# Attention: 1/sum applied by a diagonal moving operand in the transposes, eight diagonals a tile made by GpSimd and VectorE

## The reference

```python
s_loc = jnp.einsum('bnqkgd,bnjkd->bkgnqj', qb, kb) * scale      # 3 blocks of 128 keys around the query block
s_loc = jnp.where(valid, s_loc, NEG_INF)
s_ctx = jnp.einsum('bnqkgd,bjkd->bkgnqj', qb, kc) * scale       # 256 context keys
s_snk = sink_logits(sink, s_loc.shape[:-1] + (1,))
p = jax.nn.softmax(jnp.concatenate([s_loc, s_ctx, s_snk], axis=-1), axis=-1)
o = einsum(p_loc, vb) + einsum(p_ctx, vc)
```

## Time and profile before

| | |
|---|---|
| median of 3 runs | 3465.7 us (3460.85 to 3466.91) |
| the profiled execution's own time | 3464.97 us |
| its span | 3463.2 us |
| PE, PEld, DVE, ACT, POOL busy | 3005.9, 2458.5, 2095.8, 1792.2, 541.9 us |
| attention stage, first score to last product | 403.6 to 597.1 us |

### The profile page before, as it was taken

How to read it: one execution, slowest core, us unless ns; L and a number is a source line. 1 busy time by engine, 2 the same in 40 slices (tenths; PEclk the granted TensorE clock), 3 DMA queues, 4 the chain that set the end, 5 groups by cost and what they waited for, 6 DMA issues and landing times. The chain is left out here.

```text
span 3463.2 us, 59847 instructions
## 1 busy us (share of the span) xinstructions
PE 3005.9 (87%) x24750; PEld 2458.5 (71%) x24750; DVE 2095.8 (61%) x2213; ACT 1792.2 (52%) x2017; POOL 541.9 (16%) x250
## 2 busy tenths in 40 slices
PE   6599887996799999999999948997929999999993
PEld 2488643452688888788888836774529999999993
DVE  0422375234566666666666645873357888888884
ACT  2411145232555555555555545884336777777773
POOL 1011043001011111210102004561030000000000
PEclk8699889997899999999999969998959999999997
DMA  7211100227778787777788621102247999999995
GB/s 327 75 37 37 55 1 21 85 91 296 274 264 273 263 275 268 259 258 264 270 274 268 239 81 52 40 31 92 93 174 272 362 380 354 354 387 358 354 353 178
DMA packets 137950, 726.07 MB, mean 210 GB/s; under 512 B 10708, under 2 KB 13524, under 8 KB 109828
## 3 DMA queue, kind: packets, MB, share of 16 engines
q1 hardware_dynamic: 125064, 684.99, 52.6%
q0 software_dynamic: 12288, 37.75, 4.6%
q10 hardware_dynamic: 384, 0.24, 0.0%
HBM read 680.90 MB, written 42.04 MB: 209 GB/s over the span
## 5 line engine op out<-in xcount | busy, mean ns | idle before, releaser
L1540 DVE TENSOR_TENSOR mixed_low<-mixed_raw,mixed_high 128x3072 fp32r<-128x3072 f32 (+1 forms) x192 | 593.0, 3092 | 358.8 <-ACT mixed_high L1474 357.8
L1474 ACT CAST mixed_high<-mixed_raw 128x3072 fp32r<-128x3072 f32 (+1 forms) x192 | 489.8, 2554 | 481.2 <-DMA mixed_raw<-in_moe 481.2
L1961 DVE TENSOR_TENSOR rows_low<-rows_raw,rows_high 128x2816 fp32r<-128x2816 f32 x188 | 581.0, 3091 | 80.2 <-ACT rows_high L1905 69.4
L1905 ACT CAST rows_high<-rows_raw 128x2816 fp32r<-128x2816 f32 x188 | 479.4, 2559 | 110.5 <-PE ps L1812 67.1
L1396 PE MATMUL ps<-mixed_high,mixed_xhi 128*128 128x384 f32 (+1 forms) x1024 | 343.7, 336 | 0.5 <-DVE mixed_low L1540 0.5
L1810 PE MATMUL ps<-rows_high,rows_xhi 128*128 128x352 f32 x1024 | 337.4, 330 | 6.0 <-issue 4.5
L1397 PE MATMUL ps<-mixed_low,mixed_xhi 128*128 128x384 f32 (+1 forms) x1024 | 329.9, 322 | 0.0
L1398 PE MATMUL ps<-mixed_high,mixed_xlo 128*128 128x384 f32 (+1 forms) x1024 | 329.9, 322 | 0.0
L1812 PE MATMUL ps<-rows_high,rows_xlo 128*128 128x352 f32 x1024 | 329.8, 322 | 0.0
L1811 PE MATMUL ps<-rows_low,rows_xhi 128*128 128x352 f32 x1024 | 329.5, 322 | 0.0
L1384 PE MATMUL ps<-mixed_raw,mixed_xc 128*32 128x96 f32 (+1 forms) x8192 | 185.3, 243 | 48.3 <-ACT mask_sb L1496 30.8
(11 more groups left out here) (288 smaller groups left out, 5936.3 us busy)
## 6 DMA issues: line engine op xcount, KB each, us to landing
rows_raw<-in_moe_rows SPq DMA_DIRECT2D x192, 1408.0 KB, 7.9
mixed_raw<-in_moe SPq DMA_DIRECT2D x144, 1536.0 KB, 6.7
ring_r<-in_ada_w SPq DMA_DIRECT2D x24, 2048.0 KB, 17.3
mixed_raw<-in_moe SPq DMA_DIRECT2D x48, 1024.0 KB, 6.5
w_raw_r<-in_ev_in SPq DMA_DIRECT2D x18, 512.0 KB, 3.3
w_raw_u<-in_od_in SPq DMA_DIRECT2D x16, 512.0 KB, 3.3
x_res<-ring_r SPq DMA_DIRECT2D x10, 512.0 KB, 2.6
x_norm<-ring_r SPq DMA_DIRECT2D x10, 512.0 KB, 2.9
```

Of the source, the lines that this page charges most:

```text
L1474: act.copy(r.high[:, p % SLOTS, 0:nj, :], r.raw[:, p % SLOTS, 0:nj, :]).then_inc(high_done, 1)
L1540: dve.tensor_tensor(r.low[:, p % SLOTS, 0:nj, :], r.raw[:, p % SLOTS, 0:nj, :], r.high[:, p % SLOTS, 0:nj, :].bitcast(F32), ALU.subtract). ...
L1905: act.copy(high[:, p % SLOTS, :], raw[:, p % SLOTS, :]).then_inc(high_done, 1)
L1961: dve.tensor_tensor(low[:, p % SLOTS, :], raw[:, p % SLOTS, :], high[:, p % SLOTS, :].bitcast(F32), ALU.subtract).then_inc(low_done, 1)
```

## The change

The rows of probabilities are not scaled any more. POOL and DVE each multiply the identity matrix by the four reciprocals of their group, a 128x128 matrix for each head, whatever the number of keys of the tile. The transpose, which had the identity as moving operand, becomes an ordinary matmul of the unscaled block with this diagonal, which transposes and scales at once. The diagonals have two buffers, so their writers wait for the last turn of tile n-2. `sums`, the places of all calls, and the order of instructions on every engine stay: POOL and DVE issue four instructions for each tile and group as before, and PE's 336 transposes stand where they stood, as matmuls.

```diff
+            self.diag = ctx.enter_context(nc.sbuf_tensor(f"diag_{name}", [P, 2 * D], F32))
...
+    diag = m.diag.rearrange("p (b v j n) -> p b v j n", b=2, v=NKV, j=QPK)
...
                     for j in range(QPK):
-                        mm = pe.transpose(m.ps[:, 4 + kv, j * P:(j + 1) * P],
-                                          probs[n % DEEP][:, kv, j, c * P:(c + 1) * P], m.ident[:, :])
+                        mm = pe.matmul(m.ps[:, 4 + kv, j * P:(j + 1) * P], probs[n % DEEP][:, kv, j, c * P:(c + 1) * P],
+                                       diag[:, n % 2, kv, j, :], start=True, stop=True)
...
                 pool.wait_ge(rsum_done, NKV * n + 1)
+                if n >= 2:
+                    pool.wait_ge(pt_done, last_piece[n - 2] + 1)
                 for j in range(QPK):
-                    row = probs[n % DEEP][:, 0, j, a:b]
-                    pool.tensor_scalar(row, row, x[:, 7, j:j + 1], None, ALU.mult).then_inc(normed[0], 1)
+                    pool.tensor_scalar(diag[:, n % 2, 0, j, :], m.ident[:, :], x[:, 7, j:j + 1], None,
+                                       ALU.mult).then_inc(normed[0], 1)
...
-            def normalise(n):
-                a, b = span(n)
+            def diagonals(n):
                 x = small[:, n % DEEP, 1]
                 dve.wait_ge(rsum_done, NKV * (n + 1))
+                if n >= 2:
+                    dve.wait_ge(pt_done, last_piece[n - 2] + 1)
                 for j in range(QPK):
-                    row = probs[n % DEEP][:, 1, j, a:b]
-                    dve.tensor_scalar(row, row, x[:, 7, j:j + 1], None, ALU.mult).then_inc(normed[1], 1)
+                    dve.tensor_scalar(diag[:, n % 2, 1, j, :], m.ident[:, :], x[:, 7, j:j + 1], None,
+                                      ALU.mult).then_inc(normed[1], 1)
```

More of the change, by code:

```diff
@@ L910, in _ @@
                 sums(0, kv)
-            normalise(0)
+            diagonals(0)
             for n in range(NT):
@@ L923, in _ @@
                     sums(n + 1, 1)
-                    normalise(n + 1)
+                    diagonals(n + 1)
 def out_stage(nc, m, d, name, layer, inT, w_dram, sources, affT):
```

## The result

| | before | changed |
|---|---|---|
| median of 20 runs | 3465.33 us | 3474.28 us |
| range | 3453.45 to 3473.6 | 3467.69 to 3482.91 |
| ratio, 95% interval | | 1.0028 [1.0020, 1.0036] |
| span of the profiled execution | 3463.2 | 3472.0 |
| attention stage, first score to last product | 403.64 to 597.11: 193.5 us | 404.56 to 604.61: 200.05 us |

The change costs 9.7 us of 3465 by the ratio (6.9 to 12.5); the two medians lie 9.0 apart. The stage that it touches is 6.6 us longer.

The account below looks back on a forecast made before the run. PE was taken as the limit from tile 1 on, with stalls at fixed places. Stretches summed to +3.3 us at 109 ns a pass, +5.3 at 112; +4.3 taken gave 3469.3 profiled, 3470 us median, range 3461 to 3480.

Parts of the forecast that it names:

- signs of being wrong: A turn above 2.0 us, or an attention stage that ends before 594 or after 604 us.
- first turn and score: Tile 0, 440.96 to 445.29, at half clock: turn grows to 3.63 us, score falls to 1.6; +0.9 us.
- tiles 1 to 3: 57.64 us become 58.98: passes add 13.1, stalls and three half-clock stretches go; +1.3 us.
- tiles 4 to 6: 49.32 us become 54.94, from 15 turns, 15 products and four scores in each tile; +5.6 us.
- tile 9: 7.9 us, mostly at half clock, become 9.2: first turn 3.63, the rest partly at full clock; +1.3 us.
- Two passes: Every turn on PE: 672 records as ordinary float32 matmuls, a turn 1.89 us instead of 1.02, 36.7 us over 42 chunks.
- One pass or four: Rivals on the turns' matmuls: one pass, about 3440 us (5%); four passes, 3540 or more (3%).
- The loads hide: Inside every turn: weight load and stream, both about 107 ns, run together, so a pass takes 109 to 112 ns.
- The slower rival: Inside every turn the second pass does not hide its load: 3477 us at 120 ns a pass, 3540 in series; 27%.
- The waits go: PE's 1.94 us copy waits and tile 1's POOL wait go; POOL waits at tiles 0 and 9 shorten about 4 and 2.
- POOL 0.60 us, DVE 0.8 us for four, biases 1.0: Scaling at 128 columns: POOL about 0.60 us each, DVE's four 0.8 instead of 2.24, six bias operations about 1.0 from 2.19.
- the rival that ordinary matmuls bring it back sooner: After the restarts at tiles 0 and 9 full clock returns sooner with matmuls: up to -5 us, 3466; 10%.

Follow-up runs that it names:

- the pause run: The kernel before with 13 copies by ACT added at the end of the attention stage, into probabilities nobody reads any more; ratio 1.0015.
- the split version: The kernel before with group 0's row scaling split between ACT and POOL; ratio 0.9944 with bias operations moved behind DVE's scaling, 0.9958 with them in their old place.

## Why the prediction was right

The forecast was 3470 us, +4.3, in a range of 3461 to 3480; measured are 3474.28 and +9.7. The sign and the mechanism hold: a second pass in every turn, against waits and half-clock stretches that go. The size is low by half. Of the 5.4 us missed 2.3 lie in the stage (6.6 for 4.3); the other 3.1 lie outside it, where the sum has no term, and that the range took them in owes nothing to the working. 3474.28 is just above the forecast's own range of 3465 to 3474, and 0.28% is beyond the 0.2% that the prediction put down as no change, an outcome that it held more likely (0.58) than a slower kernel (0.36). One of its own signs of being wrong came true, too, by a little: the stage ends at 604.61, after 604, because it starts 0.9 us later than before and is 6.6 us longer; when the kernel ran again it ended at 603.62. Point by point, stage against stage:

| stretch | forecast | measured |
|---|---|---|
| start to first turn | -4.1 | -4.2 |
| first turn and score | +0.9 | +1.5 |
| rest of tile 0 | -1.5 | -1.3 |
| tiles 1 to 3 | +1.3 | +2.7 |
| tiles 4 to 6 | +5.6 | +6.9 |
| tile 7, tile 8 | +1.3, -1.5 | +1.6, -1.3 |
| tile 9 | +1.3 | +0.6 |
| sum (forecast at 109 ns a pass) | +3.3 | +6.6 |

- **Two passes:** right, 672 records. A turn was mis-sized by a little: 1.98 us instead of 1.89, above the 1.89 to 1.93 that was to show the mechanism and below the 2.0 that would have spoken against it. The starts at 485.22 and 486.78 in the turn that begins at 485.00 are 14 passes apart, between 111 and 112 ns each, where the forecast's 109 ns for 16 passes makes 0.04 us less; the other 0.05 are the turn's fixed part, 0.20 where I had taken 0.15 over from the transposes. The 0.09 us in 42 turns make 3.8 us, a little more than the gap between +3.3 and +6.6. The prediction's own numbers for 112 ns don't agree with each other: 37.6 us of passes has the eight added passes alone at 112, while +5.3 needs all sixteen (672 x 3 ns = 2.0 us more).
- **One pass or four:** neither rival came; each written matmul of the turns has two records.
- **The loads hide:** right, even where load and stream are equally long: 106 ns of load and 107 of stream come to 111 to 112 ns a pass. The slower rival's mechanism (120 ns) did not come; its side did, by the turn's size and by what lies outside the stage.
- **The waits go:** right, all of them from tile 1 to tile 7, with 1.0 of clock there. At tile 0 the wait is 1.16 us instead of 5.34, at tile 9 3.08 instead of 5.35.
- **POOL 0.60 us, DVE 0.8 us for four, biases 1.0:** measured 0.604, 0.88 and 0.96.
- **The clock:** the rival that ordinary matmuls bring it back sooner has no support. PE's work goes at full pace again from 600.69 on, 4.6 us after the restart at tile 9 (before: 5.7), but at tile 0 only 5.8 us after it (before: 4.3), which is most of the 0.6 us missed there. The 3.4 us at tile 9 of the pause run, with the transposes and the wait of the kernel before (5.7), show how far this differs with nothing changed ahead of it. Tile 9 of the changed kernel:

```profile
596.10 3.25 PE L772 MATMUL ps<-diag_r,A_r 128*128 128x128 f32 x16 [3.08 <-POOL diag_r L855]
...
600.69 2.05 PE L772 MATMUL ps<-diag_r,A_r 128*128 128x128 f32 x16
602.67 1.94 PE L784 MATMUL ps<-ring_r,C_first 128*64 128x512 f32 x8
```

The first turn and score of the changed kernel, with the clock in the third column from the right (0.50 in the turn, 0.59 in the score):

```profile
437.69:441.40 3.71, 3.71 (x16) 3.49 (x16) 0.46 (x2) 1.59 (x5) 0.00 (x0) 0.50 0.01 2
441.40:443.51 2.11, 2.11 (x14) 1.60 (x13) 0.69 (x1) 0.71 (x2) 0.00 (x0) 0.59 0.00 0
```

- **Not in the prediction:** that POOL's scaling was a second wait behind DVE's of the same length. It changes nothing in the sum, since the diagonals shorten both waits, but a forecast for one of them alone goes wrong by it, as mine for the moved bias operations did (10 to 15 us forecast, 2.3 measured in the stage).

## What to carry to other kernels

Moving work into TensorE's operand is free only where TensorE waits anyway: count the passes that an ordinary float32 matmul makes where a transpose makes one, and price them against the waits they replace, which here were 40 us of passes against some 34 of waiting and slow clock. Before paying on the engine that bounds the stage, look for one with idle time: half of group 0's scaling on ScalarE, with the bias operations moved, made the stage 20 us shorter and kept the single pass. And when a wait is to be removed, look at what else ends within a microsecond of it.

## What the runs showed of the hardware

- A float32 matmul of the full array with 128 moving columns takes two passes of 111 to 112 ns each at full clock in the changed kernel's turns, with its 128-column weight loads hidden; a transpose is one pass of 109 ns.
- DVE operations on SBUF took longer while POOL scaled rows in SBUF. The six bias operations took 0.96 us with POOL idle, 2.19 with POOL at work throughout and 1.62 with POOL at work for nine tenths of them; only some of the six are slowed (0.41, 0.59 and 0.72 us for 0.16), the others keep their time. Four scalings of 128x640 took 1.94 us with POOL idle (in the split version), 2.24 with POOL at work for the first 0.5 us and 3.50 beside it for most of their time, and POOL's own four then took 7.98 instead of 7.46. DVE's maxima, which read PSUM, took 0.82 us in both cases.
- After a wait of PE of 1 to 5 us at tiles 0 and 9 it took 3.4 to 5.8 us until its work went at full pace again, with transposes or ordinary matmuls. The same instructions after the same wait took 5.7 us in one execution and 3.4 in another; none of these runs orders the differences.

The scalings with POOL idle, DVE in order of time in the split version:

```profile
485.60 1.94 DVE L914 TENSOR_SCALAR A_r<-A_r,C_first 128x640 f32<-128x640 f32 x4
```
